# Four column groups of 32 in the rounds that two experts share 96 to 32

## The reference

```
comb = sum(one_hot(eid, 32) * top_p[..., None], axis=1) * p_sel   # 2 experts of one group per token
for e in range(N_EXPERTS):                                        # 32
    hdn = silu(xt @ w_gate[e]) * (xt @ w_up[e])                   # (T, 1024) @ (1024, 256), twice
    y = y + comb[:, e:e + 1] * (hdn @ w_down[e])                  # (T, 256) @ (256, 1024)
```

## Time and profile before

| | before |
|---|---|
| median of 3 runs | 1174.32 us (1172.41 to 1176.85) |
| profiled execution | 1172.66 us, its span 1170.8 us |
| mean granted TensorE clock | 0.972 of 2.4 GHz |
| TensorE matmul busy | 1095.2 us, 94% |
| VectorE, ScalarE, POOL busy | 33%, 26%, 25% |
| moved by DMA | 181.15 MB, 155 GB/s over the span |
| expert stage | 664.5 us to the end |

### The profile page before, as it was taken

One profiled execution on the slowest core, in us unless ns is written; L12 is line 12 of the kernel. 1 busy time (PEld: TensorE's weight loads), 2 busy tenths in 40 slices (PEclk: granted clock), 3 DMA queues, 4 the chain that ended last, 5 costly groups with the idle time before them and its releaser, 6 DMA issues.

```text
span 1170.8 us, 14072 instructions
## 1 busy us (share of the span) xinstructions
PE 1095.2 (94%) x5279; PEld 620.7 (53%) x5279; DVE 381.9 (33%) x924; ACT 303.1 (26%) x694; POOL 297.4 (25%) x390
## 2 busy tenths in 40 slices
PE   4899999999999998799997799999999999999995
PEld 4798878877887777578775422222222222222221
DVE  4415332532353256684337301111211111111112
ACT  4433443344334433432221110111111111111111
POOL 1113222323232221442220201132322222323132
PEclk9999999999999999799997699999999999999998
DMA  7121111111111223345537765666666666657320
GB/s 244 33 86 36 48 45 58 36 37 52 43 36 52 63 86 124 126 138 183 179 134 296 310 258 222 268 260 241 261 236 263 234 251 235 261 227 292 134 81 21
DMA packets 82438, 181.15 MB, mean 155 GB/s; under 512 B 19035, under 2 KB 52379, under 8 KB 70082
## 3 DMA queue, kind: packets, MB, share of 16 engines
q1 hardware_dynamic: 65034, 151.25, 35.3%
q0 software_dynamic: 16416, 25.73, 6.6%
q10 hardware_dynamic: 920, 3.27, 0.8%
HBM read 166.73 MB, written 47.55 MB: 183 GB/s over the span
## 4 chain that ended last, share of the span: by engine, by line
PE 87%; DVE 5%; issue 3%; ACT 2%; POOL 1%; DMA 1%; SPq 0%; POOLq 0%; DVEq 0%; ACTq 0%
PE pj L2041 27%; PE pj L1007 24%; PE pj L2083 13%; PE pj L1096 8%; PE pj L1073 4%; PE pj L1058 3%; PE tp L2021 2%; PE tp L1047 1%; PE pj L1229 1%; PE pj L2064 1%; PE pj L1902 1%; PE tp L1036 1%; DMA xt<-in_x_prompt 1%; PE tp L1019 1%; PE tp L1030 0%
## 5 line engine op out<-in xcount | busy, mean ns | idle before, releaser
L2041 PE MATMUL pj<-e_raw,xT 128*64 128x512 f32 (+1 forms) x1024 | 315.1, 607 | 0.0
L1007 PE MATMUL pj<-n_hi,w_hi 128*128 128x350 f32 (+1 forms) x576 | 197.9, 344 | 3.6 <-DVE n_lo L1327 3.6
L1007 PE MATMUL pj<-n_lo,w_hi 128*128 128x350 f32 (+1 forms) x576 | 187.7, 326 | 0.0
L1007 PE MATMUL pj<-n_hi,w_lo 128*128 128x350 f32 (+1 forms) x576 | 186.8, 324 | 0.0
L2041 PEld LDWEIGHTS pj<-e_raw,xT 128*64 128x64 f32 (+1 forms) x1024 | 59.9, 122 | 219.1 <-issue 213.3
L2083 PE MATMUL pj<-e_raw,hT 128*32 128x512 f32 (+1 forms) x512 | 163.7, 605 | 1.9 <-ACT hT L2071 1.9
L1007 PEld LDWEIGHTS pj<-n_hi,w_hi 128*128 128x128 f32 x576 | 108.8, 189 | 35.4 <-issue 33.6
L1007 PEld LDWEIGHTS pj<-n_hi,w_lo 128*128 128x128 f32 x576 | 109.1, 189 | 0.9 <-issue 0.8
L1007 PEld LDWEIGHTS pj<-n_lo,w_hi 128*128 128x128 f32 x576 | 109.2, 190 | 0.6
L693 POOL TENSOR_TENSOR w_lo<-w_raw,w_hi 128x1024 fp32r<-128x1024 f32 x21 | 50.2, 2390 | 199.9 <-ACT w_hi L770 199.9
L1289 DVE CUSTOM_DVE_ANT_0 sc<-pj,strip 128x512 f32<-128x512 f32 (+5 forms) x120 | 60.9, 543 | 117.6 <-PE pj L1073 76.6
(11 more groups left out here) (277 smaller groups left out, 1271.7 us busy)
## 6 DMA issues: line engine op xcount, KB each, us to landing
e_raw<-in_w_up SPq DMA_DIRECT2D x32, 1024.0 KB, 7.8
e_raw<-in_w_gate SPq DMA_DIRECT2D x32, 1024.0 KB
e_raw<-in_w_down SPq DMA_DIRECT2D x32, 1024.0 KB, 7.7
w_raw<-in_w_in SPq DMA_DIRECT2D x24, 512.0 KB, 3.8
wo_raw<-in_w_out SPq DMA_DIRECT2D x8, 512.0 KB, 5.8
k_page<-in_cache_k SPq DMA_DIRECT2D x16, 256.0 KB, 3.3
residual<-h_sb SPq DMA_DIRECT2D x8, 512.0 KB, 4.1
normed<-hn SPq DMA_DIRECT2D x8, 512.0 KB, 2.6
```

The lines of the kernel that those rows point to most:

```text
L1007: ins = pe.matmul(pj[g % 2][:, 0:tn], ws[w][:, P * k:P * (k + 1)], x[:, k, t0:t0 + tn], start=(m == 0), stop=(m == 23))
L2041: ins = pe.matmul(gu_bank[r % 2][a:b, :].rearrange("p (q f) -> p q f", q=2), xT[:, r % 2, k, a:b], e_raw[n % RD][:, 0:2, FF * k:FF * (k + ...
```

## The change

A round is cut into pieces of 64 only if both its halves belong to one expert each. Otherwise all its pieces are of 32. Rounds 1, 4, 7, ... stay as they are (two pieces of 64). Rounds 0, 3, ... had pieces 64, 32, 32 and rounds 2, 5, ... had 32, 32, 64; both now have four of 32, two or three of which belong to the same expert. The buffers, the waits and all other engines' programs are the same. A round's first product still clears its part of the accumulator and its last one still signals.

```diff
         def pieces(r):
 
-            runs, q = [], 0
-            while q < 4:
-                n = (4 * r + q) // 3
-                size = 2 if q % 2 == 0 and (4 * r + q + 1) // 3 == n else 1
-                runs.append((n, 32 * q, 32 * (q + size)))
-                q += size
-            return runs
+            owner = [(4 * r + q) // 3 for q in range(4)]
+            width = 2 if owner[0] == owner[1] and owner[2] == owner[3] else 1
+            return [(owner[q], 32 * q, 32 * (q + width)) for q in range(0, 4, width)]
```

## The result

The changed kernel takes 1010.88 us (median of 4, 1009.72 to 1012.07), the kernel before 1175.18 beside it: ratio 0.8604, 95% interval 0.8583 to 0.8625. The forecast was 974 with a range up to 1010, so the time lies 0.9 us above the range. The direction was right; the gain is 164 us and not the 201.7 of the sum for TensorE. So the question is what took 37 us.

The account below looks back on a forecast made before the run. The prediction took TensorE to bound the kernel, half its array columns idle in three-piece rounds. Savings of 201.7 us from 1172.7 gave 971.0; 3 us added for transfers and POOL made 974 us, range 964 to 1010.

Parts of the forecast that it names:

- the sum for TensorE: Savings on TensorE's chain through the expert stage, added piece by piece: 201.7 us, leaving 971.0 us by TensorE alone.
- A four-piece step takes 0.86 us: Gate/up and down steps of shared rounds: four 32-wide pieces run together in 0.86 us, where three-piece steps took 1.985.
- the merged step at 857.80: Old trace: two 32-wide gate/up pieces and two 32-wide down pieces of the round before ran together in 0.99 us.
- rival 4: Only two column groups run at once on TensorE in a steady stream: 1.72 us a step, 1129 us; chance 0.05.
- rival 5: The four pieces run one after another on TensorE: 3.44 us a step, 1452 us, slower; chance 0.03.
- rival 2: Instruction issue binds TensorE: a step of 0.95 to 1.10 us, 988 to 1017 us in all; chance 0.13.
- the router row: Old trace: sixteen router products with their loads took 1.13 us, 35 ns per instruction, faster than the 54 ns needed.
- POOL's round, 12.3 us: POOL's iteration from scatter to gather's end stays 12.3 us, level with the new 12.2 us round, about 6 us left.
- rival 3: POOL's round binds: scatter lands 1 to 2 us later under a full queue, 989 to 1010 us; chance 0.05.
- Transfers, "just in time" at 408 GB/s: Weight loads at 408 GB/s: last expert's gate/up weights land at 934, round 23 asks for them at 940.
- rival 1: Transfers bind: sustained rate nearer 361 than 408 GB/s once the queue is never empty, 974 to 1001 us; chance 0.17.
- the count from the whole: Weight traffic from 655.7 on: 114.3 MB, 280 us at 408 GB/s, last expert's down weights land at 939.

## Why the prediction was right on TensorE and wrong on the time

- **A four-piece step takes 0.86 us, from the merged step at 857.80.** Right. Loads come in fours every 0.43 us in every shared round; rival 4 (two groups at a time) and rival 5 (one after another) are out. The records are 1,280 on L2037 and 640 on L2079.
- **Instructions come fast enough.** Right, rival 2 is out: 16 per 0.86 us, 54 ns each, with no gap, over whole rounds. The Trainium skill's 62 ns on each MATMUL (TensorE: Matmul & The Clock Gate, "What happens when you issue a matmul") can't hold here for loads and matmuls alike; for matmuls alone, 107 ns each here, the trace doesn't decide it. The prediction has the router row below that figure, but its 35 ns count loads and matmuls alike; by the matmul it is 71 ns, above it.
- **The sum, 201.7 us, 971.0 for TensorE.** Right: 974.3 where half of the weights stay away. It holds at the upper clock level, though; TensorE's standing still brought four spells at the lower one, some 7 us, which the prediction has no term for.
- **POOL's round, 12.3 us, "level with TensorE".** This step failed. It took the 9.7 us from scatter to gather over into the new kernel. That row was read beside a queue that was full for some us and then empty; the change itself closed those gaps. The scatter then took 12.3 us to land (median), POOL's round grew to 14.1 us, and hy's gather took 8.7 for the 4.1 it had. The prediction named this as rival 3, gave it 0.05, and put the growth of the landing at 1 to 2 us; it was 2.6. Its range of 989 to 1010 ends 0.9 us below the measured time. Over 21 rounds the 1.8 us more than the 12.3 are 38 us. Its signs came: POOL waits for the scatter (88.8 us of 260) and L2089, VectorE's zs, for hy (38.9).
- **Transfers, "just in time" at 408 GB/s.** Also off, though hidden behind the first. The rate was nearly right: 415 GB/s over 100 us without the scatter's wait (720 to 820), 395 to 398 over 260 us, not the 361 of rival 1 (the changed kernel's own 364 stands at a share of 0.93). The landing was not: the estimate that a weight load lands 9 to 10 us after its issue was made for a queue with three loads in it; with 4 KB descriptors and the queue never empty, gate weights took 19 to 21. And the count from the whole asked only for round 23. Expert 29's weights, needed in round 21 together with expert 28's, are late earlier, as in each round with r mod 3 = 0. These are in the 17 us between 990.9 and 974.3, together with the three spells at the lower clock that the 4 KB kernel still has from 680 to 940 (again some 7 us, an estimate as above).
- **The two are not a sum.** Without the scatter's wait the time is 993.6, with 4 KB descriptors 990.9, with both 989.8. The first leaves hy's landing in the chain of waits (37.3% from 640 on), the other two the gate weights (24.9% and 24.7% from 664 on). Of the 37 us, 20 went with the split loads; the other 17 are the weights' bytes and what hangs on them (5.3 MB less took away 13.8, half the weights all of them).
- **The sign and the chance of faster (0.96).** Right. The range held no room for both bounds at once: its upper end took rival 3's price from an estimate that was itself read before the queue was full. Of the two conditions under which the prediction called itself fallen, the first didn't come about (a step was 0.86 us), and the second, less than 400 GB/s from a full queue, is a close call (415 over 100 us, 395 to 398 over 260). It had none on how late a transfer lands, which is where it fell.

What isn't settled: that the DMA engines give POOL's queue and SP's queue turns by descriptor was not seen. It would explain the landing of hy (16.6 to 8.2 us at equal traffic). The Trainium skill (DMA: Bandwidth & Descriptors, "Queues, rings and completion order") has each engine going round its queues packet by packet, a packet being some 9 to 17 descriptors. So by that page a turn is longer than one descriptor, and the halved issue could count as much as the halved descriptor; no run here has one without the other. The two-load experiment shows that the depth of the queue counts too, and the one without the sample output that a simple count of turns doesn't explain all.

## What to carry to other kernels

When a change shortens the engine that sets the pace by a third, divide every transfer's bytes by the new time before trusting any latency of the old trace. A landing time read where the queue was empty a third of the time was too short here, and what waits for it in an in-order queue pays the difference every round. Where small indirect transfers share the DMA engines with a bulk stream, how finely the bulk is split is a knob of its own: here going from 8 to 4 KB descriptors (loads of 1 MB to 512 KB) was worth 20 us of 1011 and cost nothing in the kernel before, and going on to 2 KB cost 7. Look in the old trace for the step that the change will make everywhere; here one merged step gave the new one's time before anything was run.

## What the runs showed of the hardware

- Four f32 products with 32 stationary columns each and four different moving operands of 512 columns run in 0.86 us together, the time of two with 64. A change between the widths costs 0.13 us (0.99 for 0.86, kernel before).
- One core moved 415 GB/s over 100 us with 8 KB descriptors (without the scatter's wait, 720 to 820) and 404 over 100 us with 4 KB (700 to 800). Over the stretch of 260 us, indirect traffic included, it was 395 with 8 KB (same kernel), 394 with 4, and 378 with 2, at shares of 0.99, 1.02 and 1.03.
- 128 gathered rows of 4 KB landed in 4.1 us beside a queue 66% busy, 8.7 in the changed kernel, 16.6 with POOL unrestrained, 8.2 there with 4 KB weight descriptors (and issues of 512 KB) in place of 8.
- A scatter of 128 such rows landed in 12.1 us in the changed kernel (664 to 960), in 9.3 with at most two loads of 1 MB in the queue at the same traffic, and in 9.1 with 4 KB descriptors.
- In the changed kernel TensorE's granted clock fell four times from 2.4 to 1.2 GHz between 680 and 940, each time after it had stood still for part of the 10 us before. In the kernel with half the weights, where it was busy for all of these 260 us, the clock stayed up.
